# One TensorE order for a fused FFN, attention and RWKV-7 block: how ready steps are chosen, and which engine carries the small copies

## The chip, the cores and the metric

One core of a Trainium2 chip runs the whole program in one launch. The metric is device time in microseconds, the median of the runs shown; smaller is better.

## What is computed

Two models in a row on 256 tokens of width 1024, all in float32. The first block is an FFN (width 2816), a mixer, an FFN and a final norm. Its mixer projects the normed rows once and uses the columns for a dilated attention (12 heads), for an RWKV-7 time mix (16 heads of 64) and for two sets of gates. Then two layers of FFN, sparse and latent attention, FFN. The change lies in the first block's mixer. Of the reference, cut to it:

```python
def token_shift(z, mu):
    prev = jnp.pad(z, ((0, 0), (1, 0), (0, 0)))[:, :-1]
    return z + (prev - z) * mu

def hybrid_mixer(h, ...):
    proj = h @ w_in
    gates = jax.nn.sigmoid(proj[..., aw + rs:] + gate_bias)
    y_attn = dilated_attention(proj[..., :aw], positions) @ attn_w_up
    y_rwkv = rwkv7_time_mix(token_shift(proj[..., aw:aw + rs], rwkv_mu), ...)
    merged = gates[..., :D_MODEL] * y_attn + gates[..., D_MODEL:] * y_rwkv
    return merged @ w_o

# rwkv7_time_mix, per head: S_t = S_{t-1} diag(w_t) + (S_{t-1} a_t) b_t^T + v_t k_t^T ;  y_t = S_t r_t
```

## The kernel before, in words

**Stages.** The stages run one after the other: ffn f1, mix1, ffn f2, final, f3, mix2, f4, f5, mix2, f6, final. Products are made of three float32r matmuls each (high and low parts, `mm3`, L1799 to L1801; in the FFNs L1857 and L1859). Weights come in chunks of up to 1 MB through three `raw` buffers; ScalarE writes the high part (`split`, L2345), VectorE the low part (L2711), in four pieces a chunk.

**How the order is made.** The class `Order` writes one list of steps ahead of time; every engine then runs its share in order, and semaphores join them. In mix1 and mix2 the function `woven` interleaves chains: the first is `dense` (weight products), the others are the recurrence's. Each chain has a time at which its next step is ready, from the table `PACE` and from `HOP`; `woven` takes the first chain in the list that is ready, so `dense` comes first as soon as its rest of 1.0 us after its last step is over. `mode` says whether TensorE's last step was of 64-wide tiles (`QUARTERS`) or not. `BLANKS` names steps ahead of which TensorE runs so many matmuls on data that nobody reads (`fill`, L1808, 256 columns each).

**mix1.** First the qkv tile 0 with the norm, then two small shifted projections (`shift`, for the LoRA columns), then the rest of qkv; then attention, interleaved with gates 0 and 1 and the shifted k, v, r projections of group pair 0; then `rwkv`. There 8 head pairs g run as chains `group`, `decay`, `rows`, `gates`; two Front and three Whole buffers are shared among them. `dense` there is: `up` (attention output times its weights), `streams(1)` (shifted k, v, r of heads 2 and 3), gate 2, `streams(2)`, gate 3, `streams(3)`, and then `wout`. `streams(G)` waits until the rows of pairs 2G-4 and 2G-3 have been used. Each g has 20 steps of 64-wide tiles: `r_lora`, `r_pairs`, `r_dm0`, `r_g0`, five `r_x`, five `r_d`, `r_w`, `r_rp`, `r_yp`, three `r_s`; and full steps such as `r_norm`, `r_wide`, `r_vb`, `r_ka`, `r_bonus`, `r_mean`, `r_var`, `r_lg`, `r_turn2`.

**Around the changed operations.** A shift: `shift_mm` on TensorE into one PSUM bank; `shift_copy` on ScalarE copies the bank into the buffer `z` one column to the right (L2452) and frees the bank; `shift_mix` on VectorE subtracts (L2831, 128x512) and adds mu times the difference (L2836, twice). `r_key` ends with a VectorE copy that spreads a norm per head over 64 columns (L2959) for TensorE's `r_wide`; `r_wide2` does the same (L3093) ahead of `r_turn2`. `r_st` scales a 128x64 state out of PSUM (L3073, VectorE), three times a pair, and `r_s` on TensorE (L2157, L2159) waits for each.

```python
def shift_copy(s, sid, n, w):
    for t in due(("pe", ("shift", sid)), ("pool", ("z0",)), z_free(sid)):
        e.wait_ge(*t)
    e.activation(z[0:w, 0:n, 1:257], bank(sid)...[0:w, 0:n, :], copy)
```

Of the kernel before, what the change touches and what calls it, by code (L numbers as in the profile page):

```python
# [24 lines left out]
CW = 2048  # L25


def plan(stages):
# [11 lines left out]
    def body(s):  # L40
# [15 lines left out]
        elif s[0] == "mix1":  # L56
# [7 lines left out]
            out += gate[0] + gate[1] + kvr[0] + [("mix1", "up", 0, 2048)] + kvr[1] + gate[2] + kvr[2] + gate[3] + kvr[3]  # L64
# [30 lines left out]
def down_after(m):  # L95

    if 5 <= m <= 8:
# [11 lines left out]
    "r_key": (("dve", 0.59),), "r_wide": (("pe", 0.25),), "r_vb": (("pe", 0.45), ("act", 0.68)),  # L109
# [4 lines left out]
    "r_rp": (("pe", 0.35), ("dve", 0.69)), "r_yp": (("pe", 0.9), ("pool", 0.1, "aside")), "r_st": (("dve", 0.22),),  # L114
    "r_s": (("pe", 0.15),), "r_ys": (("act", 0.43),), "r_mean": (("pe", 0.43), ("dve", 0.36)), "r_sq": (("act", 0.36),),
    "r_var": (("pe", 0.3), ("dve", 0.1), ("pool", 1.0)), "r_wide2": (("dve", 0.32),), "r_lg": (("pe", 0.88),),
# [32 lines left out]
         "r_ka", "r_bonus", "r_pairs"}  # L149
HOP = {"pe": 0.3, "act": 0.1, "dve": 0.1, "pool": 0.15}  # L150
# [144 lines left out]
class Dry:  # L295
# [44 lines left out]
    def max(self, *a, **k):  # L340
        return self
# [3180 lines left out]
```

## Time and profile before

| | us |
|---|---|
| median of 3 runs | 1875.25 (1875.21 to 1876.46) |
| the profiled execution, its own time | 1876.75 |
| its span | 1875.0 |
| TensorE busy in the span | 1846.3 (98%) |
| VectorE, ScalarE, GpSimd busy | 1200.3, 1014.8, 91.2 |
| share of the last-ending chain on TensorE | 91% |
| blanks (L1808) over the whole span | 317 matmuls |

The profiled execution is 1.5 us over the median. Busy is the union of an engine's instructions; TensorE's matmuls are pipelined, so time lost between two kinds of matmul still counts as busy, and so do blanks. mix1's recurrence lies between 338 and 583 us of the span, its attention ahead of it, its output products behind it to about 640 us.

### The profile page before, as it was taken

The numbers are of one execution on the slowest core, as the hardware profiler recorded it, in microseconds if no ns is written. First come the engines' busy times: TensorE is split into PE (matmuls) and PEld (weight loads), VectorE is DVE, ScalarE is ACT, GpSimd is POOL, SyncE is SP. The second block draws the span as 40 slices with busy tenths as digits, with TensorE's granted clock in tenths as the row PEclk, the third lists the DMA queues.
The fourth block names the chain that finished last, engine by engine and source line by source line (L and its number), as shares of the span: only waits on it lengthen the run. The fifth ranks groups of instructions, "written<-read, shape, count | busy, mean of one in ns | idle before, by whom it ended". The sixth has DMA issues, their size and how long they took to land.

```text
span 1875.0 us, 31192 instructions
## 1 busy us (share of the span) xinstructions
PE 1846.3 (98%) x12765; PEld 1569.5 (84%) x12765; DVE 1200.3 (64%) x2485; ACT 1014.8 (54%) x2074; POOL 91.2 (5%) x187
## 2 busy tenths in 40 slices
PE   8999999999999999999999999999999999999998
PEld 7888888888887888888888887888888888878887
DVE  5666545767766557665666665667566767566565
ACT  5565455534523556555655765556555656655554
POOL 0000000211210000010001000000000000000000
PEclk9999999999999999999999999999999999999999
DMA  6556443222214356535652333556355634334552
GB/s 244 181 202 234 159 157 113 101 88 94 76 53 159 125 193 233 202 109 184 230 208 85 132 135 113 182 204 241 114 181 200 242 98 133 137 113 168 201 185 109
DMA packets 42719, 296.31 MB, mean 158 GB/s; under 512 B 4832, under 2 KB 4960, under 8 KB 10576
## 3 DMA queue, kind: packets, MB, share of 16 engines
q1 hardware_dynamic: 41184, 288.48, 43.5%
q0 software_dynamic: 1392, 5.83, 0.9%
q8 instruction: 101, 1.65, 0.4%
q14 instruction: 42, 0.34, 0.1%
HBM read 293.25 MB, written 1.05 MB: 157 GB/s over the span
## 4 chain that ended last, share of the span: by engine, by line
PE 91%; DVE 5%; ACT 2%; POOL 1%; issue 1%; DMA 1%; SPq 0%; POOLq 0%; DVEq 0%; ACTq 0%
PE PS L1857 22%; PE PS L1799 16%; PE PS L1801 15%; PE PS L1800 15%; PE PS L1859 11%; PE PS L1808 1%; PE PS L2100 1%; PE PS L2302 1%; PE PS L1834 1%; PE PS L2214 1%; DVE wlo L2711 1%; PE PS L1993 1%; PE PS L2266 1%; PE PS L2258 1%; PE PS L2081 1%
## 5 line engine op out<-in xcount | busy, mean ns | idle before, releaser
L2711 DVE TENSOR_TENSOR wlo<-raw,whi 128x512 fp32r<-128x512 f32 (+5 forms) x788 | 612.7, 823 | 191.7 <-ACT whi L2345 185.1
L1857 PE MATMUL PS<-xhl,whi 128*128 128x512 f32 x1728 | 612.9, 398 | 0.0
L2345 ACT ACTIVATE whi<-raw 128x512 fp32r<-128x512 f32 (+5 forms) x788 | 531.2, 731 | 144.1 <-PE PS L1801 144.0
L1859 PE MATMUL PS<-xhl,wlo 128*128 128x256 f32 x1728 | 484.8, 281 | 0.0
L1857 PEld LDWEIGHTS PS<-xhl,whi 128*128 128x128 f32 x1728 | 324.7, 188 | 79.1
L1859 PEld LDWEIGHTS PS<-xhl,wlo 128*128 128x128 f32 x1728 | 326.2, 189 | 2.1
L1799 PE MATMUL PS<-whi,yh 128*128 128x512 f32 (+2 forms) x572 | 224.9, 393 | 0.5 <-DVE yl L3115 0.3
L1801 PE MATMUL PS<-whi,yl 128*128 128x512 f32 (+2 forms) x572 | 221.8, 388 | 0.0
L1800 PE MATMUL PS<-wlo,yh 128*128 128x512 f32 (+2 forms) x572 | 221.7, 388 | 0.0
L1799 PE MATMUL PS<-whi,xhl 128*128 128x512 f32 (+4 forms) x480 | 191.5, 399 | 1.1 <-ACT arena L2546 0.7
L2796 DVE TENSOR_TENSOR arena<-arena,PS 128x256 f32<-128x256 f32 x216 | 90.3, 418 | 159.2 <-ACT arena L2415 159.2
L1801 PE MATMUL PS<-whi,xhl 128*128 128x512 f32 (+4 forms) x480 | 180.1, 375 | 0.0
L1800 PE MATMUL PS<-wlo,xhl 128*128 128x512 f32 (+4 forms) x480 | 179.9, 375 | 0.0
L1799 PEld LDWEIGHTS PS<-whi,yh 128*128 128x128 f32 x572 | 107.4, 188 | 26.0 <-issue 3.1
L1801 PEld LDWEIGHTS PS<-whi,yl 128*128 128x128 f32 x572 | 107.4, 188 | 23.1
L1800 PEld LDWEIGHTS PS<-wlo,yh 128*128 128x128 f32 x572 | 107.5, 188 | 19.5
L2412 ACT ACTIVATE arena<-arena 128x256 f32<-128x256 f32 x108 | 45.1, 418 | 124.7 <-DVE arena L2796 124.7
L1799 PEld LDWEIGHTS PS<-whi,xhl 128*128 128x128 f32 x480 | 90.6, 189 | 17.7 <-issue 2.4
L1801 PEld LDWEIGHTS PS<-whi,xhl 128*128 128x128 f32 x480 | 90.5, 188 | 14.0
L2418 ACT ACTIVATE yh<-arena 128x256 fp32r<-128x256 f32 x108 | 45.1, 418 | 102.3 <-DVE arena L2800 102.3
L1800 PEld LDWEIGHTS PS<-wlo,xhl 128*128 128x128 f32 x480 | 90.8, 189 | 11.3
L2804 DVE TENSOR_TENSOR yl<-arena,yh 128x256 fp32r<-128x256 f32 x108 | 46.0, 425 | 52.3 <-ACT yh L2418 52.3
(269 smaller groups left out, 2400.6 us busy)
## 6 DMA issues: line engine op xcount, KB each, us to landing
raw<-wall SPq DMA_DIRECT2D x249, 1024.0 KB, 4.9
raw<-wall SPq DMA_DIRECT2D x12, 768.0 KB, 4.3
raw<-wall SPq DMA_DIRECT2D x8, 968.0 KB, 4.9
raw<-wall SPq DMA_DIRECT2D x4, 896.0 KB, 4.7
arena<-ebias POOLq DMA_DIRECT2D x2, 768.0 KB, 4.7
raw<-wall SPq DMA_DIRECT2D x2, 720.0 KB, 4.1
raw<-wall SPq DMA_DIRECT2D x2, 640.0 KB, 4.5
X<-x SPq DMA_DIRECT2D x2, 512.0 KB, 5.9
```

Source lines behind the costliest of these rows:

```text
L1799: e.matmul(o, wa, xa, start=first, stop=False)
L1800: e.matmul(o, wa, xb, start=False, stop=False)
L1801: return e.matmul(o, wb, xa, start=False, stop=last)
L1808: e.matmul(PS[:, i, 0:256], still[:, 0:128], still[:, :], start=True, stop=True)
L1857: e.matmul(b, hi[:, c0:c0 + 128], xhl[:, k, :, :].rearrange("p a t -> p (a t)"), start=(k == 0), stop=False, skip_group_check=True)
L1859: p = e.matmul(b[:, 0:256], lo[:, c0:c0 + 128], xh[:, k, :], start=False, stop=(k == 7), skip_group_check=True)
L2345: e.activation(whi[slot_of(i)][:, c].bitcast(F32R), raw[i % 3][:, c], copy).then_inc(*M.sig("whi", ("split", i, q)))
L2412: e.activation(g, g, ACT.Silu).then_inc(*M.sig("act", ("silu", s, m)))
L2418: e.activation(hbuf(m)[0], g, copy).then_inc(*M.sig("act", ("hh", s, m)))
L2711: e.tensor_tensor(wlo[slot_of(i)][:, c], raw[i % 3][:, c], whi[slot_of(i)][:, c].bitcast(F32), ALU.subtract).then_inc(*M.sig("wlo", *[("ha ...
L2796: e.tensor_tensor(o, o, bank(("gu", s, m, n))[:, 0:256], ALU.add).then_inc(*M.sig("dve", (key, s, m), ("free", ("gu", s, m, n))))
L2804: e.tensor_tensor(hl, g, hh.bitcast(F32), ALU.subtract).then_inc(*M.sig("dve", ("hl", s, m)))
```

## The change

It has seven parts.

1. `woven` keeps the name of each chain's last step; among the chains that are ready it prefers one whose next TensorE step is of the tile that TensorE is in (`NEXTQ` names the last steps after which a 64-wide one comes).
2. `dense` of `rwkv` follows the table `DENSE`: k, v, r of pair group 1, `up`, groups 2 and 3, gates 2 and 3. The chunks of weights are loaded in that order.
3. The shift has no buffer `z`: ScalarE writes (1 - mu) times the bank straight into its place, in two instructions; VectorE adds mu times the bank one column to the right, out of PSUM, and frees the bank. The wait for the place (`kzv_free`) moves from VectorE to ScalarE. 1 - mu is made once (`m1_begin`); the memset of `z` goes.
4. `r_st` moves from VectorE to ScalarE.
5. The two spreads (in `r_key`, and `r_wide2`) move from VectorE to ScalarE.
6. `PACE` has new estimates for these steps.
7. `BLANKS` has other entries: 146 matmuls in mix1 for 195, none for 4 in the first FFN, 50 for 49 in each mix2.

```diff
+DENSE = (('kvr', 1, 1.0), ('up', 0, 1.0), ('kvr', 2, 1.0), ('kvr', 3, 1.0), ('gate', 2, 1.0), ('gate', 3, 1.0))
...
-            out += gate[0] + gate[1] + kvr[0] + [("mix1", "up", 0, 2048)] + kvr[1] + gate[2] + kvr[2] + gate[3] + kvr[3]
+            out += gate[0] + gate[1] + kvr[0]
+            for what, n, _ in DENSE:
+                out += {"up": [("mix1", "up", 0, 2048)], "gate": gate[n], "kvr": kvr[n]}[what]
...
-    "shift_mm": (("pe", 1.54),), "shift_copy": (("act", 0.54),), "shift_mix": (("dve", 1.47),),
+    "shift_mm": (("pe", 1.54),), "shift_copy": (("act", 0.7),), "shift_mix": (("dve", 0.86),),
...
+NEXTQ = {"r_dt", "r_dm0", "r_xc", "r_dd", "r_w", "r_rp", "r_yp", "r_st", "r_s", "r_scaled", "r_bonus"}
...
-    ('proj', 0, 'gh', 0, 4): 4, ('turn_x', 1, 0, 0): 4, ('proj', 1, 'qkv', 1, 0): 4, ('proj', 1, 'gate', 0, 0): 13,
-    ('att_qk', 1, 0): 15, ('att_turn', 1, 1, 1, 0): 3, ('att_out', 1, 3, 0): 8, ('up', 1, 0, 0, 0): 20,
-    ('r_vb', 1, 0): 8, ('r_vb', 1, 1): 9, ('r_g0', 1, 1): 5, ('r_g0', 1, 2): 5, ('r_d', 1, 5, 1): 6,
-    ('r_g0', 1, 6): 6, ('r_dm0', 1, 6): 13, ('r_turn2', 1, 5): 5, ('r_d', 1, 7, 3): 11, ('r_x', 1, 7, 5): 3,
-    ('r_s', 1, 7, 1): 4, ('r_s', 1, 7, 2): 4, ('r_s', 1, 7, 3): 4, ('r_mean', 1, 7): 4, ('r_var', 1, 7): 8,
-    ('r_turn2', 1, 7): 5, ('wout', 1, 3, 1, 0): 19, ('wo', 1, 1, 0, 1): 6, ('wo', 1, 3, 0, 0): 3,
+    ('turn_x', 1, 0, 0): 4, ('proj', 1, 'gate', 0, 0): 13, ('att_qk', 1, 0): 15, ('att_out', 1, 3, 0): 8,
+    ('r_vb', 1, 0): 14, ('r_d', 1, 4, 1): 7, ('r_dm0', 1, 5): 6, ('r_s', 1, 4, 3): 4, ('r_g0', 1, 7): 9,
+    ('r_d', 1, 7, 4): 5, ('r_d', 1, 7, 5): 4, ('r_s', 1, 7, 1): 4, ('r_s', 1, 7, 2): 3, ('r_s', 1, 7, 3): 3,
+    ('r_mean', 1, 7): 4, ('r_var', 1, 7): 7, ('r_turn2', 1, 7): 6, ('wout', 1, 3, 1, 0): 19,
+    ('turn_merged', 1, 4, 0): 4, ('wo', 1, 1, 0, 1): 7, ('proj', 4, 'gh', 0, 0): 20, ('turn_x', 5, 0, 0): 4,
...
-            c = next((c for c in able if max(c[1], c[3]) <= self.now), None) or min(able, key=lambda c: max(c[1], c[3]))
+            now = [c for c in able if max(c[1], c[3]) <= self.now]
+            c = next((c for c in now if (c[4] in NEXTQ) == self.mode), None) or (now and now[0]) or min(able, key=lambda c: max(c[1], c[3]))
...
+            c[4] = self.steps[-1][0] if len(self.steps) > n else c[4]
...
         self.do("shift_copy", s, sid, n, w)
-        self.bank.give(sid)
         yield 1
         self.do("shift_mix", s, sid, n, w)
+        self.bank.give(sid)
...
             def shift_copy(s, sid, n, w):
-                for t in due(("pe", ("shift", sid)), ("pool", ("z0",)), z_free(sid)):
+                o, b = dest(sid), bank(sid)
+                for t in due(("pe", ("shift", sid)), ("dve", ("less",)), *kzv_free(sid)):
                     e.wait_ge(*t)
...
+                for j in range(n):
+                    e.activation(o[0:w, j, :], b[0:w, j * 256:(j + 1) * 256], copy, scale=less(mus(sid)[j])[0:w]).then_inc(
+                        *M.sig("act", ("shift", sid)))
...
+            def r_st(s, g, c):
+                W_, q, tt = WH[slot("whole", g)], c % 2, c // 2
+                for t in due(("pe", ("s", g, c) if c else ("yp", g)), ("act", ("pc", g))):
+                    e.wait_ge(*t)
+                e.activation(W_.ST[:, c, :], bank(("YP", g, q))[:, 128 + tt * 64:192 + tt * 64], copy,
+                             scale=W_.st[:, 24 + c:25 + c]).then_inc(*M.sig("act", ("ST", g, c)))
+
+            def r_wide2(s, g):
+                W_ = WH[slot("whole", g)]
+                for t in due(("pool", ("rsd", g))):
+                    e.wait_ge(*t)
+                e.activation(u4(W_.B), W_.st[:, 4:8].unsqueeze(2).to_broadcast([128, 4, 64]), copy).then_inc(
+                    *M.sig("act", ("wide2", g)))
...
             def shift_mix(s, sid, n, w):
-                o = dest(sid)
-                for t in due(("act", ("shift", sid)), *kzv_free(sid), COLS):
-                    e.wait_ge(*t)
-                e.tensor_tensor(o[0:w, 0:n, :], z[0:w, 0:n, 0:256], z[0:w, 0:n, 1:257], ALU.subtract).then_inc(
-                    *M.sig("dve", ("shifted", sid)))
+                o, b = dest(sid), bank(sid)
+                for t in due(("act", ("shift", sid)), COLS):
+                    e.wait_ge(*t)
                 for j in range(n):
...
+                    e.scalar_tensor_tensor(o[0:w, j, 1:256], b[0:w, j * 256:j * 256 + 255], col("mu", mus(sid)[j])[0:w],
+                                           o[0:w, j, 1:256], ALU.mult, ALU.add).then_inc(
+                        *M.sig("dve", ("mix", sid), *[("free", sid)] * (j == n - 1)))
```

## Rows read from the trace of the kernel before

**Rows 1.** the page's part 1: busy time, share, instructions
```profile
PE 1846.3 (98%) x12765; PEld 1569.5 (84%) x12765; DVE 1200.3 (64%) x2485; ACT 1014.8 (54%) x2074; POOL 91.2 (5%) x187
```

**Rows 2.** stretches of mix1: length, busy us (x instructions) by engine, PEclk, DMA
```profile
338.00:510.00 172.00, 168.80 (x2906) 144.40 (x2906) 129.69 (x340) 76.71 (x188) 40.64 (x59) 1.00 0.26 90
510.00:548.00 38.00, 35.69 (x1008) 30.98 (x1005) 29.09 (x97) 11.39 (x33) 6.67 (x14) 1.00 0.04 11
```

**Rows 3.** TensorE in order of time, 13 to 18 us
```profile
16.98 0.74 PE L1808 MATMUL PS<-still 128*128 128x256 f32 x4 [1.53 <-ACT still L2336]
17.56 0.39 PE L1799 MATMUL PS<-early,xhl 128*128 128x512 f32 x1
```

**Rows 4.** VectorE in the same stretch
```profile
14.78 1.28 DVE L2711 TENSOR_TENSOR early<-raw,early 128x512 fp32r<-128x512 f32 x2
```

**Rows 5.** TensorE around the first qkv tile after the lora shifts
```profile
223.37 0.63 PE L1808 MATMUL PS<-still 128*128 128x256 f32 x4
224.19 0.50 PE L1799 MATMUL PS<-whi,xhl 128*128 128x512 f32 x1 [0.19 <-DVE wlo L2711]
```

**Rows 6.** TensorE before the up product
```profile
330.38 2.63 PE L1808 MATMUL PS<-still 128*128 128x256 f32 x20
333.28 0.47 PE L1799 MATMUL PS<-whi,yh 128*128 128x512 f32 x1 [0.27 <-DVE small L2936]
```

**Rows 7.** TensorE around 64-wide steps, 391 to 397 and 567 to 569 us
```profile
395.81 0.67 PE L2109 MATMUL PS<-arena 64*64 64x128 f32 x16
396.30 0.38 PE L2081 MATMUL PS<-arena 64*64 64x32 f32 x16
...
566.92 0.39 PE L1800 MATMUL PS<-wlo,yh 128*128 128x512 f32 x1
567.14 0.39 PE L1801 MATMUL PS<-whi,yl 128*128 128x512 f32 x1
567.46 0.67 PE L2109 MATMUL PS<-arena 64*64 64x128 f32 x16
568.06 0.50 PE L1799 MATMUL PS<-whi,yh 128*128 128x512 f32 x1
568.39 0.40 PE L1800 MATMUL PS<-wlo,yh 128*128 128x512 f32 x1
```

**Rows 8.** TensorE in order of time: first and last 64-wide stretch of the recurrence
```profile
339.28 0.70 PE L1981 MATMUL PS<-arena 64*128 64x256 f32 x4
...
575.62 0.33 PE L2159 MATMUL PS<-arena 64*64 64x64 f32 x4
```

**Rows 9.** blanks (L1808) of two stretches: TensorE busy us (x instructions)
```profile
338.00:600.00 262.00, 19.55 (x125) 16.14 (x125) 1.00 0.24 84
```

**Rows 10.** TensorE's waits, 330 to 600 us: in total, times, longest
```profile
PE PS L1993 <- DVE arena L2959: 1.2, 1, 1.2
```

**Rows 11.** VectorE by line, 330 to 600 us: busy, mean ns, idle before
```profile
L2831 DVE TENSOR_TENSOR arena<-arena 128x512 f32<-128x512 f32 x10 | 6.9, 691 | 5.9 <-ACT arena L2452 5.9
L3073 DVE TENSOR_SCALAR arena<-PS,arena 128x64 f32<-128x64 f32 x24 | 6.7, 281 | 10.7 <-PE PS L2159 5.5 <-PE PS L2146 5.0
...
L2959 DVE COPY arena<-arena 128x256 f32<-128x256 f32 x8 | 2.5, 314 | 0.0
```

**Rows 12.** ScalarE by line, 330 to 600 us
```profile
L2452 ACT ACTIVATE arena<-PS 128x512 f32<-128x512 f32 x10 | 6.0, 599 | 27.7 <-PE PS L1801 27.7
...
L2573 ACT ACTIVATE arena<-PS 128x128 f32<-128x128 f32 x16 | 3.6, 275 | 11.8 <-PE PS L2159 11.7
...
L2585 ACT ACTIVATE yh<-arena 128x256 fp32r<-128x256 f32 x8 | 3.3, 414 | 16.1 <-DVE arena L3108 16.1
...
L2542 ACT ACTIVATE arena<-PS 128x256 f32<-128x256 f32 x8 | 3.1, 384 | 4.0 <-PE PS L1993 3.7
...
L2532 ACT ACTIVATE arena<-arena 128x4 f32<-128x4 f32 x8 | 1.6, 195 | 0.0
```

**Rows 13.** one stretch at a lower granted clock (PEclk)
```profile
1134.00:1138.00 4.00, 4.00 (x19) 3.48 (x17) 1.21 (x2) 0.90 (x2) 0.00 (x0) 0.57 0.72 305
```

More of the change, by code:

```diff
@@ L610, in woven @@
         self.epochs.append(len(self.steps))
-        live, idle = [[g, self.now, False, 0.0] for g in (steady,) + chains], 0
+        live, idle = [[g, self.now, False, 0.0, ""] for g in (steady,) + chains], 0
         dense = live[0]
@@ L1010, in dense @@
         def dense():
-            self.acc(s, "up")
-            yield from self.down("up", s, lambda j: ("mix1", "up", 0), [0], True)
-            self.do("gate_attn", s)
-            self.acc_free(s, "up")
-            yield from streams(1)
-            yield from self.gate(s, 2)
-            yield from streams(2)
-            yield from self.gate(s, 3)
-            yield from streams(3)
+            for what, n, self.rest in DENSE:
+                if what == "up":
+                    self.acc(s, "up")
+                    yield from self.down("up", s, lambda j: ("mix1", "up", 0), [0], True)
+                    self.do("gate_attn", s)
+                    self.acc_free(s, "up")
+                elif what == "gate":
+                    yield from self.gate(s, n)
+                else:
+                    yield from streams(n)
             while not set(range(6)) <= out:
@@ L1574, in build @@
         KZV[0] = {q: sp.take(2, 256) for q in "kvr"}
-        LW, z = sp.take(1024), sp.take(2, 257)
+        LW = sp.take(1024)
         sp = Space()
@@ L1718, in dest, with kzv_free, less @@
             return KZV[sid[1] % 2][sid[0]]
-        def z_free(sid):
-            q, G = sid
-            if q == "l":
-                return G and ("dve", ("mix", ("l", 0)))
-            if q == "k":
-                return "dve", ("mix", ("r", G - 1) if G else ("l", 1))
-            return "dve", ("mix", ({"v": "k", "r": "v"}[q], G))
+        def kzv_free(sid):
+            if sid[0] == "l":
+                return []
+            return marked("kzv", sid[1] - 2) if sid[1] >= 2 else marked("attn", 1) if sid[1] else marked("norm", 1)
+        def less(j):
+            return small[:, 16 + j:17 + j]
         def mus(sid):
@@ L2001, in r_wide @@
             def r_wide(s, g):
-                for t in due(bank_free(("r_wide", g)), ("dve", ("wide", g))):
+                for t in due(bank_free(("r_wide", g)), ("act", ("wide", g))):
                     e.wait_ge(*t)
@@ L2151, in r_s @@
                 b = bank(("YP", g, q))
-                for t in due(("dve", ("Ph", g)), ("dve", ("ST", g, c - 1))):
+                for t in due(("dve", ("Ph", g)), ("act", ("ST", g, c - 1))):
                     e.wait_ge(*t)
@@ L2182, in r_turn2 @@
             def r_turn2(s, g):
[L2183 removed]
+                for t in due(bank_free(("r_turn2", g)), ("act", ("wide2", g))):
                     e.wait_ge(*t)
@@ L2566, in r_w, with r_key @@
                     *M.sig("act", ("w", g), *freed("r_w", g)))
+            def r_key(s, g):
+                F_ = FR[slot("front", g)]
+                for t in due(("pool", ("nrm", g))):
+                    e.wait_ge(*t)
+                e.activation(u4(F_.wide), F_.st.unsqueeze(2).to_broadcast([128, 4, 64]), copy).then_inc(
+                    *M.sig("act", ("wide", g)))
+            def r_st(s, g, c):
[10 more added lines that the diff above has]
+                    *M.sig("act", ("wide2", g)))
             def r_ys(s, g):
@@ L2956, in r_key @@
                 e.scalar_tensor_tensor(F_.kp, F_.kp, 1.0, k3, ALU.add, ALU.mult).then_inc(*M.sig("dve", ("kp", g)))
-                for t in due(("pool", ("nrm", g))):
-                    e.wait_ge(*t)
-                e.tensor_copy(u4(F_.wide), F_.st.unsqueeze(2).to_broadcast([128, 4, 64])).then_inc(
-                    *M.sig("dve", ("wide", g)))
             def r_scaled(s, g, part):
@@ L3067, in r_rp @@
                     *M.sig("dve", ("Ph", g), ("free", ("RP", g, 0))))
-            def r_st(s, g, c):
-                W_, q, tt = WH[slot("whole", g)], c % 2, c // 2
-                for t in due(("pe", ("s", g, c) if c else ("yp", g)), ("act", ("pc", g))):
-                    e.wait_ge(*t)
-                e.tensor_scalar(W_.ST[:, c, :], bank(("YP", g, q))[:, 128 + tt * 64:192 + tt * 64],
-                                W_.st[:, 24 + c:25 + c], None, ALU.mult).then_inc(*M.sig("dve", ("ST", g, c)))
             def r_mean(s, g):
```

45 lines of the change are left out of this document (17 added, 28 removed).

## The prediction

> **What bounds the kernel now.** I read the engines' busy time first: TensorE is busy 98% of the span [rows 1], so only what shortens TensorE's own line counts, or what lets it wait less. Next the stretches of mix1: while the recurrence runs beside products (338 to 510 us) TensorE is busy 168.80 of 172 us, and in the part where no products are left (510 to 548 us) 35.69 of 38; VectorE is busy three quarters of both, ScalarE 45% and 30% [rows 2]. VectorE is thus the second engine and ScalarE has room. Busy TensorE hides three kinds of loss, and the change aims at all: open waits, blanks, and changes between 64-wide and full steps. Open waits are small: the longest of the recurrence is 1.2 us, on the spread L2959 [rows 10]. Between 338 and 600 us blanks take 19.55 us in 125 matmuls, 0.156 us each with the entry to their batch [rows 9]; a blank more in a batch costs 0.12 to 0.15 us (20 in 2.63) [rows 6]. Changes of tile are read from start times.
>
> **The price of a 64-wide stretch.** Full fp32r matmuls of 512 columns stand 0.23 us apart (566.92 to 567.14 and its like). From the one at 567.14 to the 64-wide step behind it 0.32 pass, so entering costs 0.09; the first full matmul after it (568.06) takes 0.33 to the next, so leaving costs 0.10 [rows 7]. The step itself, L2109, takes 0.60 when it stands alone (567.46 to 568.06) and 0.49 when another 64-wide step follows (395.81 to 396.30) [rows 7]: 0.11 of waiting for the last ones to drain. A stretch less saves 0.09 + 0.10 + 0.11 = **0.30 us**. In the order of starts I count 88 stretches with the 160 64-wide steps of the recurrence, from 339.28 to 575.62 us [rows 8]: 1.8 steps each.
> The Trainium skill ("TensorEngine Tiling (Array Packing)", Key Properties) says that a change of tiling mode drains the TensorE; it gives no figure, and the trace agrees. By that rule every merged pair would save the whole 0.30, whatever stands beside it, and the sum would be the one below.
>
> **The change part by part.**
> *Start.* In the first FFN the four blanks wait for a constant from ScalarE until 16.98, and the product behind them starts at 17.56 [rows 3]; the half chunk it needs was cut by 14.78 + 1.28 = 16.06 on VectorE [rows 4]. Without blanks it starts about 16.1: **-1.4 us**. The chunks behind it are fed ahead of TensorE, which shows no wait after that point before the tile's end; if one of them is late, the gain is 0.
> *First qkv tile.* Four blanks end at 224.00 and the product still waits 0.19 for the low part [rows 5]. VectorE's queue had the subtraction of the shift ahead of it, 0.69 us [rows 11], which goes; ScalarE's two copies add at most 2 x 0.384 - 0.599 = 0.17 ahead of the high part [rows 12]. **-0.5**, ends 0 and -0.8.
> *up.* After the turn of the attention's output, TensorE runs 20 blanks and waits until 333.28, 2.90 us from 330.38, for that output's low part [rows 6]. In the new order shifted k of group 1 stands there, which needs only normed rows and weights; its chunk takes the place of up's in the loading. The attention's end is then covered by 18 us of products. **-2.9**, other end 0 if k's chunk is late.
> *Order of ready steps.* Stretches of 1.8 steps can at best become about 3 (three Whole buffers, so three pairs under way, one ready step each): 160/3 = 53 stretches, 35 less, -10.5. At worst no second step is ready at a choice: 88 and 0. A 1.4 us product step lets all three chains become ready, which speaks for the far half, the dependence of every step on VectorE or ScalarE for the near one. I take the middle, 18 less: 18 x 0.30 = **-5.4**.
> *Gates last.* 22 us of gate products move from between the shifts to the end, where the stretch without products stands with its blanks and waits; they cover it, while the shifts, closer together, start the later pairs sooner. What of the blanks goes: 106 for 125 between 338 and 600 us (up's 20 lie ahead of it), 19 x 0.12 = **-2.3**; ends 0 (the stall is still there, uncovered) and 19 x 0.156 = -3.0. Three more go in the attention and three in wo: **-0.5**. The chain of the last pair (its `r_s`, mean, variance, turn, then wout with 19 blanks) stays bare in either order.
> *Shift without z.* Per shift VectorE loses 0.69 [rows 11], over ten shifts of the stretch 6.9; its two other operations stay. ScalarE gains 0.17. The bank is freed by VectorE and not by ScalarE, about 1 us later, in 8 banks; cover is that products rest 1.0 us between steps. The wait for the place goes ahead of ScalarE's copy; behind it stand the high parts of weights and the recurrence's copies. Nothing before shows VectorE waiting at L2831 for anything but ScalarE's copy (5.9 us in all) [rows 11], so I cost it at 0.
> *Spreads and states.* VectorE loses 24 x 0.281 and 16 spreads of about 0.31 [rows 11], 11.8 us; with the shifts 18.6 us of the 194 that it is busy there. For a 128x64 copy out of PSUM ScalarE has no row: between 0.195 (128x4) and 0.275 (128x128) [rows 12], against 0.281; I take 0.25, equal on the chain. A spread on ScalarE is nearest to its 128x256 copy inside SBUF, 0.414 [rows 12]: 0.1 longer than now, 16 times, bare only for the last pair. What VectorE no longer has in its queue ends most of the wait for L2959 (1.2) [rows 10]: **-1.0**, ends 0 and -1.2. Added on the other side: `r_st` or a spread behind a piece of the weights' high part on ScalarE, which takes 0.6 as the bank copy does; counted in the range.
> The Trainium skill ("VectorE: DVE Perf Modes", the TRN2 errata) speaks against the spreads' move: its fixed cost for a source in SBUF is 224 cycles at 1.2 GHz on ScalarE and 58 at 0.96 GHz on VectorE. By it a spread would be 0.40 us there and 0.33 here, an estimate from that page; the trace has 0.414 and 0.314 and agrees in direction, and 16 x 0.1 us on the path would turn the sum by 1.6 us at most.
> *Two mix2 stages.* One blank more each: **+0.2**.
>
> **Sum.** 1.4 + 0.5 + 2.9 + 5.4 + 2.3 + 0.5 + 1.0 - 0.2 = 13.8 us off. The profiled execution took 1876.75 (span 1875.0), 1.5 over the median; the savings are inside the span and I take them from the median: 1875.25 - 13.8 = **1861.5**.
>
> **Rivals.**
> *A: the chains set the time.* Each pair's 20 steps depend on one another; if TensorE has less to do per step, it waits more, and the merged stretches and dropped blanks come back as waits. For it: already now no products are left at 510 to 548 us and 2.3 us are open there [rows 2]. Against: with products TensorE is open only 3.2 of 172 us [rows 2]. Only start, qkv and up stay: 4.8 off, **1870.5**.
> *B: the order rule merges nothing* (the change does not do what it says), because seldom two steps are ready; all else holds: 13.8 - 5.4 = 8.4 off, **1866.9**.
> *C: slower, products run out in the middle.* `streams(2)` and `streams(3)` wait for rows of earlier pairs, and no gate stands between them now. TensorE then runs recurrence steps alone. Such a stretch wastes 2.3 us open and about 5.3 in 44 blanks (0.12 each) in 38, a fifth. Before it is 38 us long; the gates at the end win these 7.6 back. If the bare stretches ahead of both shift groups last L us, the loss is 0.2 L; with no merging and no dropped blank (1870.5 as in A) the point of decision is 0.2 L - 7.6 = 4.8, L = 62 us. With 80 us the time is 1870.5 - 7.6 + 16 = **1879**. For it: the group of heads 4 and 5 can only be shifted once pair 1's rows are used; against: the shifts themselves are 17 us each.
> Also, one stretch of 4 us runs at a mean granted clock of 0.57 [rows 13], in a mix2 stage that the change leaves as it is; the lower level (1.2 GHz) there followed TensorE's small attention steps and a wait. It costs six matmuls 0.2 us more each; it may go or come again: 1.2 us either way, for the range.
>
> **How the numbers follow.** About 0.2% (3.75 us) is what a measurement of this kernel can tell from no change. Forecast 0.65, A 0.16, B 0.10, C 0.09. The forecast's own range: merging at its far end and blanks and start at theirs 5.1 + 0.9 more, the clock 1.2: 1854; down to near B, 1868. Eight in ten takes in A with its bounds: 1853 to 1872. Faster (below 1871.5): all of the forecast, 0.09 of A's 0.16, 0.06 of B's 0.10 (its blanks can fail with it): 0.80. Same: 0.07 + 0.04 = 0.11. Slower: C, 0.09.
>
> **What the changed profile would show.** Right: no blank ahead of the first FFN's fifth k; a shift product at 330 us where blanks stood; clearly under 88 stretches of 64-wide steps, about 70; 0.30 for each that went; gate products beside the recurrence's last pairs; VectorE 18 us less busy and ScalarE some 14 more; spreads at 0.41 on ScalarE. Wrong: open waits of TensorE in the recurrence over 10 us in sum (A); a count near 88 (B); tens of microseconds with no fp32r matmul before the third shift group (C); ScalarE's shift copy waiting for GpSimd, VectorE or a chain's rows; a product waiting for a chunk that is not cut.

## The result, and the profile after

The changed kernel takes **1862.39 us** (median of 5 runs, 1861.97 to 1873.29) against 1876.05 us (1875.21 to 1877.22) for the kernel before in the same comparison: a ratio of 0.9939 [0.9924, 0.9953], 13.7 us less. The forecast was 13.8 us less, 1861.5.

The execution that was profiled with it is the longest of the five, 1873.29 us (span 1871.5), 11 us over its median, so its trace alone would tell another story than the time. The same kernel went to the chip once more (`e1_again`: 1861.78 us in the profiled execution, span 1860.0), and that trace is the one to lay beside the kernel before. Every line number of TensorE's program is 8 higher than before: products L1807 to L1809, blanks L1816. First the page's busy times of `e1_again`, columns as in [rows 1].

```profile
PE 1833.8 (99%) x12714; PEld 1562.2 (84%) x12714; DVE 1182.0 (64%) x2432; ACT 1029.0 (55%) x2127; POOL 89.2 (5%) x186
```

TensorE is 12.5 us less busy, VectorE 18.3 less, ScalarE 14.2 more. Next the recurrence, which from here on is the stretch from the turn of the attention's output (L1826 before, L1834 now) to the last group of `wout`. The view is the stretches, columns as in [rows 2]: the kernel before, then `e1_again`, then the first trace of the changed kernel with the stretch in it that ran at half clock.

```profile
330.03:584.23 254.20, 247.98 (x4240) 211.35 (x4239) 179.67 (x485) 102.91 (x251) 50.69 (x78) 1.00 0.24 85
```
```profile
327.80:570.60 242.80, 237.35 (x4197) 205.17 (x4197) 163.51 (x435) 116.96 (x301) 48.81 (x78) 1.00 0.25 88
```
```profile
329.20:580.80 251.60, 246.29 (x4197) 212.34 (x4196) 163.49 (x435) 117.03 (x301) 48.87 (x78) 0.96 0.24 86
526.20:546.60 20.40, 20.33 (x268) 16.84 (x265) 8.37 (x24) 5.62 (x14) 2.41 (x4) 0.50 0.17 60
```

So 11.4 of the 15.0 us between the spans are saved here: 254.2 us became 242.8 (the window's edges are rounded; from start to start it is 242.7, as in the table below). In the first trace of the changed kernel the same 4197 matmuls took 251.6, because for 20.4 us of them the granted clock was 0.50 (1.2 GHz). Half of 20.4 is 10.2, and 251.6 - 242.8 is 8.8.

The start, and the place where `up`'s 20 blanks stood [rows 3, 6], TensorE in order of time in `e1_again`:

```profile
14.72 0.40 PE L1809 MATMUL PS<-early,xhl 128*128 128x512 f32 x1
15.80 0.50 PE L1807 MATMUL PS<-early,xhl 128*128 128x512 f32 x1 [0.68 <-DVE early L2742]
...
222.03 0.50 PE L1807 MATMUL PS<-whi,xhl 128*128 128x512 f32 x1 [0.16 <-DVE wlo L2742]
...
327.85 0.60 PE L1834 MATMUL PS<-C,arena 128*128 128x128 f32 x4
328.20 0.36 PE L1807 MATMUL PS<-xhl,whi 128*128 128x256 f32 x1
```

The fifth k starts at 15.80 (17.56 before), with nothing ahead of it but the wait for the cut chunk; the first qkv tile at 222.03 (224.19). Behind the attention's turn a shift product starts after 0.35 us, at 328.20, where the next product stood 3.25 us behind (330.03 to 333.28).

Merged steps, TensorE in order of time in `e1_again`:

```profile
399.26 0.59 PE L2174 MATMUL PS<-arena,C 128*128 128x256 f32 x2
399.78 1.08 PE L2154 MATMUL PS<-arena 64*64 64x64 f32 x53
400.65 0.25 PE L2101 MATMUL PS<-arena 64*64 64x32 f32 x2
...
400.96 0.63 PE L2108 MATMUL PS<-arena 64*64 64x32 f32 x15
401.53 0.61 PE L1995 MATMUL PS<-C,arena 128*128 128x2 f32 x4
```

Two 64-wide steps of different pairs stand side by side here: `r_yp` (L2154) and an `r_d`, which has two groups of matmuls (L2101, L2108). Counted in the order of starts, the 160 64-wide steps stand in **70 stretches** where there were 88, and 21 of these are a single step where 45 were.

The end of the products, TensorE in order of time: the last product of the shifts and the first of `wout` before, then the last of the gates and the first of `wout` in `e1_again`.

```profile
508.37 0.28 PE L1801 MATMUL PS<-xhl,wlo 128*128 128x256 f32 x1
...
548.48 0.58 PE L1799 MATMUL PS<-whi,yh 128*128 128x512 f32 x1
```
```profile
510.97 0.40 PE L1809 MATMUL PS<-whi,xhl 128*128 128x512 f32 x1
...
534.34 0.59 PE L1807 MATMUL PS<-whi,yh 128*128 128x512 f32 x1
```

For 40.1 us no product stood beside the last pairs' steps; now it is 23.4.

What the moved operations cost, ScalarE by line from 325 to 590 us, then VectorE (columns as in [rows 11]):

```profile
L2462 ACT ACTIVATE arena<-PS,small 128x256 f32<-128x256 f32 x20 | 8.4, 469 | 18.9 <-PE PS L1809 18.9
L2589 ACT ACTIVATE arena<-PS,arena 128x64 f32<-128x64 f32 x24 | 7.5, 312 | 24.6 <-PE PS L2167 13.2 <-PE PS L2154 11.4
...
L2596 ACT ACTIVATE arena<-arena 128x256 f32<-128x256 f32 x8 | 3.3, 413 | 5.7 <-POOL arena L3357 5.6
...
L2582 ACT ACTIVATE arena<-arena 128x256 f32<-128x256 f32 x8 | 3.3, 411 | 0.7 <-POOL arena L3339 0.7
```
```profile
L2865 DVE SCALAR_TENSOR_TENSOR arena<-PS,C,arena 128x255 f32<-128x255 f32 x20 | 8.7, 474 | 5.6 <-ACT arena L2462 5.5
```

The shift's copies (L2462) wait for TensorE alone, 18.9 us in all, and never for a place or for VectorE; the mix (L2865) waits 5.6 us, all but 0.1 of it for them, as L2831 did before (5.9) [rows 11].

### The profile page after: what moved, and what is told of

Same layout as the page of the kernel before. It is cut to its first block, busy times and chain, and to the rows that moved or that the text cites. A ratio compares the mean times of both kernels' runs of the same rounds, so it can differ in the third digit from the quotient of the medians.

```text
span 1871.5 us, 31118 instructions
## 1 busy us (share of the span) xinstructions
PE 1844.7 (99%) x12714; PEld 1570.5 (84%) x12714; DVE 1181.7 (63%) x2432; ACT 1029.5 (55%) x2127; POOL 89.4 (5%) x186
## 4 chain that ended last, share of the span: by engine, by line
PE 91%; DVE 4%; ACT 3%; DMA 1%; issue 1%; POOL 1%; SPq 0%; POOLq 0%; DVEq 0%; ACTq 0%
PE PS L1865 22%; PE PS L1807 16%; PE PS L1809 15%; PE PS L1808 15%; PE PS L1867 11%; PE PS L1816 1%; PE PS L2108 1%; DVE wlo L2742 1%; PE PS L2310 1%; PE PS L1842 1%; PE PS L2222 1%; PE PS L2089 1%; PE PS L2274 1%; PE PS L2266 1%; PE PS L2101 1%
## 5 line engine op out<-in xcount | busy, mean ns | idle before, releaser
L1807 PE MATMUL PS<-whi,yh 128*128 128x512 f32 (+2 forms) x572 | 225.8, 395 | 0.4 <-DVE yl L3127 0.3
L1808 PE MATMUL PS<-wlo,yh 128*128 128x512 f32 (+2 forms) x572 | 222.4, 389 | 0.0
L1809 PE MATMUL PS<-whi,yl 128*128 128x512 f32 (+2 forms) x572 | 222.4, 389 | 0.0
L1807 PE MATMUL PS<-whi,xhl 128*128 128x512 f32 (+4 forms) x480 | 191.4, 399 | 0.3 <-DVE wlo L2742 0.3
L1809 PE MATMUL PS<-whi,xhl 128*128 128x512 f32 (+4 forms) x480 | 179.9, 375 | 0.0
L1808 PE MATMUL PS<-wlo,xhl 128*128 128x512 f32 (+4 forms) x480 | 179.6, 374 | 0.0
L1807 PEld LDWEIGHTS PS<-whi,yh 128*128 128x128 f32 x572 | 107.8, 189 | 26.2 <-issue 2.6
L1809 PEld LDWEIGHTS PS<-whi,yl 128*128 128x128 f32 x572 | 107.8, 188 | 23.2
L1808 PEld LDWEIGHTS PS<-wlo,yh 128*128 128x128 f32 x572 | 107.9, 189 | 19.7
L1807 PEld LDWEIGHTS PS<-whi,xhl 128*128 128x128 f32 x480 | 90.6, 189 | 16.4 <-DVE wlo L2742 1.4
L1809 PEld LDWEIGHTS PS<-whi,xhl 128*128 128x128 f32 x480 | 90.3, 188 | 14.1
L1808 PEld LDWEIGHTS PS<-wlo,xhl 128*128 128x128 f32 x480 | 90.8, 189 | 11.3
L2423 ACT ACTIVATE arena<-PS 128x256 f32<-128x256 f32 x108 | 40.7, 377 | 70.7 <-PE PS L1867 70.7
```

What stands on the lines that cost most here:

```text
L1807: e.matmul(o, wa, xa, start=first, stop=False)
L1808: e.matmul(o, wa, xb, start=False, stop=False)
L1809: return e.matmul(o, wb, xa, start=False, stop=last)
L2423: e.activation(up, bank(("gu", s, m, 1))[:, 256:512], copy).then_inc(*M.sig("act", ("up2", s, m)))
```

## The experiments

Times are medians, ratios are against the kernel before, run beside it on the same chip (medians 1875.5 to 1876.0 us; `e1` to `e4`, `e5` to `e8` and `e9` to `e12` each had a chip of their own). A trace shows one execution out of four or more: those of `e3` and `e10` took 2.3 and 4.2 us less than their median, that of `e8` 3.2 us more. For every run I read the recurrence in the same six numbers. **Length** and the time at **half clock** are read from the trace (PEclk 0.50 by stretches); **open** is all of TensorE's waiting in the recurrence in gaps over 0.15 us, in front of steps and of blanks and inside steps (the sum of the view of its waits); **blanks** are matmuls of the filler; **stretches** are runs of 64-wide steps, both counted in the order of starts; **bare** is the sum of the stretches of 11 us and more in which no product step starts.

```
kernel                        time    length  half clock  open  blanks  stretches  bare
before                        1876.05  254.2     0         5.3    139      88      54.8
after, first trace            1862.39  251.6    20.5       5.0     95      70      44.2
e1  after again               1862.37  242.7     0         5.1     95      70      37.3
e2  no rule                   1876.75  256.7    10.2       9.3     95      85      49.6
e3  old product order         1893.23  270.9    27.3      18.8     95      72      66.8
e4  r_st, spreads back        1880.75  261.4    20.4      15.3     88      70      60.2
e5  no rule, blanks fitted    1868.11  248.6     0         3.8    106      89      49.1
e6  old order, blanks fitted  1886.88  267.3    23.9       7.2    154      82      62.5
e7  back, blanks fitted       1875.79  256.3     0         6.4    161      74      56.7
e8  no blanks before r_       1865.60  248.7    20.4      12.9     19      61      37.7
e9  before + rule             1887.81  266.3    17.1      15.2    133      74      67.0
e10 before + copies           1888.82  265.5    17.1      11.4    128      85      66.5
e11 before + product order    1886.14  264.4    13.7      12.3    123      86      63.5
e12 warmer start              1862.82  242.9     0         4.9     95      70      37.1
```

One sum fits nearly all rows: length = 205 + open + 0.12 per blank + 0.30 per stretch + half of the time at half clock. The two prices are those of the prediction, and 205 is what is left of a row on average: 254.2 - 5.3 - 16.7 - 26.4 = 205.8 in `before`, 242.7 - 5.1 - 11.4 - 21.0 = 205.2 in `e1`. Over all rows it misses by 1.0 us at most, but for `e7`, which is 3.4 longer. Fitted freely to the other thirteen rows (least squares, open taken as it is), the prices come out at 0.12 for a blank, 0.32 for a stretch and 0.47 of the time at half clock, so the rows bear the prediction's two prices out.

**Bare** is no term of that sum, since it holds waits, blanks and stretches itself, but it sorts the kernels nearly as their times do: 37 us in the changed kernel and without the pairs' blanks, 49 to 50 without the rule, 55 before, 57 and 60 with the copies back, 62.5 to 67 in all others; the first trace, with its half-clock stretch, has 44. It follows the times and doesn't show what makes them.

### The changed kernel again

The kernel is unchanged, five runs.

> The changed kernel once more, nothing edited. Its median was 1862.39 us while its one profiled execution took 1873.29 with 20.4 us at half clock in the recurrence. If that half-clock stretch is chance, this run gives 1862 +- 1 and a profile without it, span near 1860.5. If it belongs to being profiled or to this order, the profile shows it again at the same place (526 to 547 us).

Measured: 1862.37 us (1861.41 to 1866.57), 0.9933 [0.9919, 0.9947]. The gain is the same on a second comparison. The long stretch at half clock and the one at the start are both absent from this trace, and one run of the five is again 4 us above the others. The stretch of the first trace therefore belongs to an execution and not to the kernel.

### Without the rule

```diff
-            c = next((c for c in now if (c[4] in NEXTQ) == self.mode), None) or (now and now[0]) or min(...)
+            c = (now and now[0]) or min(...)
```

> The changed kernel with the old choice among ready chains (first in the list). Its order has 85 stretches of 64-wide steps where the changed kernel has 70. Theory (each stretch costs 0.30 us): 15 x 0.30 = 4.5 us more, 1866.9. Rival A (chains set the time, merged stretches come back as waits): no change, 1862 to 1863, with TensorE's open waits in the recurrence smaller by what the stretches cost more.

Measured: 1876.75 us (1873.5 to 1879.24), 1.0004 [0.9995, 1.0013]; the whole gain is gone. Stretches go from 70 to 85, worth 4.5 us, yet the time goes up by 14.4. The trace has the rest: 4.2 us more open, and two stretches at half clock that `e1` doesn't have, worth 5.1. The three make 13.8 of the 14.0 us that the recurrence is longer.

```profile
431.00:434.40 3.40, 3.40 (x32) 3.06 (x25) 2.04 (x4) 1.42 (x3) 1.56 (x3) 0.50 0.00 0
540.30:547.10 6.80, 6.63 (x71) 5.14 (x64) 3.99 (x9) 3.24 (x8) 0.31 (x1) 0.50 0.00 0
```

The blanks in this kernel are still those written for the order that the rule gives; in another order they stand ahead of steps that are ready, and the waits are elsewhere. So the run doesn't price the rule alone, which is why `e5` follows.

### With the products' old order

```diff
-DENSE = (('kvr', 1, 1.0), ('up', 0, 1.0), ('kvr', 2, 1.0), ('kvr', 3, 1.0), ('gate', 2, 1.0), ('gate', 3, 1.0))
+DENSE = (('up', 0, 1.0), ('kvr', 1, 1.0), ('gate', 2, 1.0), ('kvr', 2, 1.0), ('gate', 3, 1.0), ('kvr', 3, 1.0))
```

> The changed kernel with the products in the old order (up, kvr 1, gate 2, kvr 2, gate 3, kvr 3); 72 stretches. Theory: the wait ahead of up is back, 2.9 us (now open, no blanks), the stretch without products is bare again, 2.3, and two stretches more, 0.6: 5.8 more, 1868.2. Rival (only up mattered, the gates' place not): 2.9, 1865.3. Rival C turned round (gates between helped): under 1865.

Measured: 1893.23 us (1890.92 to 1896.56), 1.0094 [1.008, 1.0108]: 31 us more than the changed kernel, and 17 more than the kernel before, which has this same order. Waits of TensorE from 327.7 to 598.7 us (in total, times, longest), and the product of `up` behind the attention's turn:

```profile
PE PS L2001 <- ACT arena L2596: 2.3, 2, 1.3
PE PS L2001 <- DVE arena L3004: 2.2, 3, 1.7
PE PS L1807 <- DVE small L2966: 2.2, 1, 2.2
PE PS L2067 <- DVE arena L3051: 1.9, 1, 1.9
PE PS L2130 <- ACT arena L2575: 1.6, 3, 0.7
```
```profile
330.50 0.47 PE L1807 MATMUL PS<-whi,yh 128*128 128x512 f32 x1 [2.15 <-DVE small L2966]
```

The wait that `up`'s 20 blanks filled [rows 6] is back as 2.15 us of open time: the third line of the waits. Another 12 us are waits of up to 1.9 us on the pairs' steps (18.8 us open for 5.1 in all), and 27.3 us run at half clock. Behind the last shift no product starts for 34.0 us, and then again for 20.5 and 12.3: the gates no longer cover the last pairs.

### r_st and the spreads back on VectorE

```diff
-            def r_st(s, g, c):
...
-                e.activation(W_.ST[:, c, :], bank(...), copy, scale=W_.st[:, 24 + c:25 + c])
+            def r_st(s, g, c):
...
+                e.tensor_scalar(W_.ST[:, c, :], bank(...), W_.st[:, 24 + c:25 + c], None, ALU.mult)
...
-                e.activation(u4(F_.wide), F_.st.unsqueeze(2).to_broadcast([128, 4, 64]), copy)
+                e.tensor_copy(u4(F_.wide), F_.st.unsqueeze(2).to_broadcast([128, 4, 64]))
```

The lines taken out are ScalarE's and those put in VectorE's. `r_wide2` likewise; `PACE` gets its old estimates for the three steps.

> The changed kernel with r_st and both spreads back on VectorE; 70 stretches as before. Theory: 1.0 us more, 1863.4, and VectorE 11.8 us busier. Rival (VectorE is the true second bound, so its relief made the merging possible): 3 us or more, 1865.5 or over. Rival (a copy on ScalarE is slower on the chain): the time falls below 1862.

Measured: 1880.75 us (1880.18 to 1882.2), 1.0028 [1.0017, 1.0039], 18 us more than the changed kernel. VectorE is 10.6 us busier in the recurrence (174.12 for 163.51), and TensorE waits for it:

```profile
PE PS L2089 <- DVE arena L3057: 2.4, 1, 2.4
PE PS L2001 <- DVE arena L3102: 2.1, 1, 2.1
PE PS L2001 <- DVE arena L2987: 1.9, 2, 1.0
PE PS L2101 <- DVE arena L3117: 1.6, 1, 1.6
PE PS L2117 <- DVE arena L3062: 1.5, 3, 0.9
```

That is a term 18 times the size that I gave it. But the stretches (70) are the same as in `e1`, so what grew is waiting (10.2 us) and half clock (20.4, worth 10.2).

### The three again, each with blanks fitted to it

The entries of `BLANKS` that lie in the recurrence are replaced in each: where that kernel's own trace shows a wait of 0.33 us or more (blanks taken away), one blank for every 0.125 us of it. From `e5`, the lines joined:

```diff
-    ('r_vb', 1, 0): 14, ('r_d', 1, 4, 1): 7, ('r_dm0', 1, 5): 6, ('r_s', 1, 4, 3): 4, ('r_g0', 1, 7): 9,
...
+    ('r_vb', 1, 0): 16, ('r_g0', 1, 3): 8, ('r_d', 1, 5, 1): 5, ('r_d', 1, 5, 5): 5, ('r_rp', 1, 5): 4,
...
```

> e2 (old choice among ready chains) with the blanks of the recurrence put where e2's own profile has TensorE waiting 0.33 us or more, one per 0.125 us. Theory after e2: its 14.4 us over the changed kernel are half-clock stretches (10.2 us long, 5.1 lost), open waits that the table didn't cover, and only 4.5 for 15 more stretches of 64-wide steps. Then blanks that fit bring the clock back: 1867.5 to 1869. Rival: the clock doesn't fall for lack of blanks, and the order alone costs 14: 1875 to 1877 again.

> e3 (products in the old order) with blanks fitted to its own profile in the same way. TensorE's waits in e3, with blanks taken away, add up to 22.5 us in the recurrence against 13.7 in e1: 8.8 more. Theory: 8.8 plus up to 3.6 for stretches, clock back: 1871 to 1875. Rival (the blanks have no part in it): 1891 to 1895 again.

> e4 (state scaling and spreads back on VectorE) with blanks fitted to its own profile. Waits with blanks taken away: 21.3 us in e4, 13.7 in e1, 7.6 more, nearly all on VectorE. Theory (VectorE is the second bound): 1862.4 + 7.6 + about 1 for stretches: 1870 to 1872. Rival 1 (as in the prediction, the copies cost 1.0 and all else in e4 was the clock): 1863.5 to 1865. Rival 2 (blanks have no part): 1880 to 1882 again.

Measured: `e5` 1868.11 us (1867.74 to 1869.78), 0.9961 [0.9948, 0.9975]; `e6` 1886.88 (1884.31 to 1887.43), 1.0056 [1.0044, 1.0069]; `e7` 1875.79 (1874.53 to 1878.58), 1.0 [0.9991, 1.0009]. `e5` came out as expected, `e6` and `e7` above their theories' ranges (1871 to 1875 and 1870 to 1872) and below the rivals in which blanks have no part. The recurrence of `e5`, `e6` and `e7`, columns as above:

```profile
328.10:576.70 248.60, 243.98 (x4208) 207.65 (x4207) 164.35 (x435) 117.79 (x301) 50.65 (x78) 1.00 0.24 87
```
```profile
328.40:595.70 267.30, 259.60 (x4256) 221.88 (x4255) 165.56 (x437) 117.49 (x302) 50.57 (x78) 0.96 0.24 84
```
```profile
329.00:585.30 256.30, 249.09 (x4263) 214.41 (x4262) 173.79 (x477) 105.92 (x262) 50.06 (x78) 1.00 0.25 88
```

Fitting alone gives back 8.6, 6.3 and 5.0 us, and in `e5` and `e7` every stretch at half clock in the recurrence is gone (PEclk 1.00). What is left over the changed kernel is the price of each part in this setting, and an upper bound: each table was fitted once, from one trace, and no run fits the changed kernel's own table anew in the same way, so part of a price can be a worse fit.

- **The rule: 5.7 us.** 19 stretches more (89 for 70) at 0.30 are 5.7; 11 blanks more (1.3) and 1.3 us less open cancel. No half clock is in the way here, and it is the prediction's price.
- **The product order: 24.5 us**, of which 59 blanks are 7.1, 12 stretches 3.6, 2.1 is open and 12.0 is half of 23.9 us at half clock. Blanks didn't cure this order: 62.5 us stay bare, and with 154 blanks it still has waits and the low clock. `e6` has the rule and the copies of the changed kernel on the product order of the kernel before, and is 11 us slower than that kernel: in the old order the two gain nothing even with blanks fitted to them once.
- **r_st and the spreads: 13.4 us**, of which 66 blanks are 7.9, 4 stretches 1.2 and 1.3 is open. The other 3 are not accounted for. `r_st` and the spreads were only moved together, so what each is worth stays open.

### Without the blanks ahead of the pairs' steps

```diff
-    ('r_vb', 1, 0): 14, ('r_d', 1, 4, 1): 7, ('r_dm0', 1, 5): 6, ('r_s', 1, 4, 3): 4, ('r_g0', 1, 7): 9,
-    ('r_d', 1, 7, 4): 5, ('r_d', 1, 7, 5): 4, ('r_s', 1, 7, 1): 4, ('r_s', 1, 7, 2): 3, ('r_s', 1, 7, 3): 3,
-    ('r_mean', 1, 7): 4, ('r_var', 1, 7): 7, ('r_turn2', 1, 7): 6,
```

> The changed kernel without the 76 blanks ahead of the recurrence's steps (those ahead of wout, wo, gates and attention stay); order and everything else the same. Theory (blanks only keep the clock up): TensorE's waits are as long as before, now open, half-clock stretches of several us come in the recurrence, 1868 to 1878. Rival (blanks cost what they hide): no half-clock stretch, and 0 to 1 us faster than 1862.4.

Measured: 1865.60 us (1862.51 to 1868.77), 0.9948 [0.9935, 0.996]: 3.2 us more than with them by the medians, though the intervals of the two ratios overlap (`e1` has 0.9919 to 0.9947); the expectation had 1868 to 1878, or no more than 1862.4. The 76 blanks cost 9.1 us of TensorE; without them 7.8 us more is open and, blanks no longer cutting them, only 61 stretches are left. At full clock this kernel would be the faster one, by an estimate that no run shows: 248.7 - 10.2 is 238.5, against 242.7. But in this trace, of the longest of its five executions, it runs 20.4 us at half clock, in four places:

```profile
341.00:344.40 3.40, 3.40 (x18) 3.40 (x17) 3.33 (x10) 2.02 (x5) 0.00 (x0) 0.50 0.54 227
392.20:399.00 6.80, 6.80 (x92) 6.07 (x91) 3.23 (x9) 1.35 (x4) 2.23 (x2) 0.50 0.02 7
453.60:457.00 3.40, 3.40 (x25) 3.27 (x21) 1.43 (x4) 2.55 (x7) 0.96 (x3) 0.50 0.02 5
569.70:576.50 6.80, 6.76 (x27) 5.95 (x28) 1.97 (x5) 0.83 (x2) 1.04 (x1) 0.50 0.00 0
```

Read this way, a blank fills a wait and shortens none, and what it is worth is the clock behind the wait: a few us in all.

### Each part alone on the kernel before

`e9` adds the rule (the line of `e2`, and `NEXTQ`), `e10` the shift without `z`, `r_st` and the spreads on ScalarE, with the old choice and the old product order, `e11` the new product order:

```diff
+            now = [c for c in able if max(c[1], c[3]) <= self.now]
+            c = next((c for c in now if (c[4] in NEXTQ) == self.mode), None) or (now and now[0]) or min(...)
```
```diff
-            yield from streams(1)
-            yield from self.gate(s, 2)
-            yield from streams(2)
-            yield from self.gate(s, 3)
-            yield from streams(3)
+            for what, n, self.rest in DENSE:
```

All three keep the old table of blanks. A blank is written only where a PSUM bank is free at that place of the order, so not all of the 139 come: 133, 128 and 123.

> The kernel before with the new choice among ready chains alone; 74 stretches of 64-wide steps for 88, its blanks as before. Theory (the parts add up, 0.30 us a stretch): 14 x 0.30 = 4.2 off, 1871.5. Rival (the parts only pay together: blanks and estimates of before don't suit the new order): 1875 to 1882, with more open waits and half-clock stretches than before.

> The kernel before with the shift without z, the state scaling and the spreads on ScalarE, and their estimates; old choice, old order of products, blanks of before. Theory of the prediction: 0.5 + 1.0 off, 1874.3. After e7 (13.4 us lost when scaling and spreads go back to VectorE) the rival is that VectorE's relief is worth the same here: 1862 to 1866. Rival 2: only in the new order, where VectorE is pressed harder, is it worth anything: 1874 to 1880.

> The kernel before with the new order of products and chunks alone (k, v, r of group 1 ahead of up; gates last), blanks of before without the 20 ahead of up, which find no free bank or no step there. Theory of the prediction: 2.9 + 2.3 off, 1870.5 or a little over, since its blanks aren't fitted. Rival (shifts closer together press VectorE, which carries 18 us more here): waits in the recurrence grow, 1876 to 1885.

Measured: `e9` 1887.81 us (1886.16 to 1891.06), 1.0068 [1.0056, 1.0081]; `e10` 1888.82 (1884.14 to 1891.67), 1.0069 [1.0055, 1.0083]; `e11` 1886.14 (1883.89 to 1886.43), 1.0054 [1.0041, 1.0066]. All three lie above the ranges of their rivals too. **Each of the three parts of a change that gains 13.7 us loses 11 to 13 when it is made alone, with the old blanks.** Waits of TensorE in the recurrence of `e9`, then of `e11`:

```profile
PE PS L1996 <- DVE arena L3096: 2.1, 1, 2.1
PE PS L1996 <- DVE arena L2981: 1.7, 3, 0.9
PE PS L2084 <- DVE arena L3111: 1.5, 1, 1.5
```
```profile
PE PS L2106 <- DVE arena L3044: 2.1, 2, 1.4
PE PS L2115 <- DVE arena L3054: 1.0, 1, 1.0
```

`e9` merges as it should (88 to 74 stretches, 4.2 us), and loses it to 10 us more open and 17.1 at half clock. `e10` has VectorE's relief and the kernel before's product order, and no gain either. `e11` alone has the short stretch behind the gates (22.9 us without a product, as 23.8 in `e1`), but two more of 15.3 and 11.6 elsewhere: the cover has moved and the chains have not come under it. And the 20 blanks of `up`, which the expectation took to be gone, run at the new place of `up`, behind a wait for the bank that they write:

```profile
370.59 2.66 PE L1814 MATMUL PS<-still 128*128 128x256 f32 x20 [0.69 <-ACT arena L2542]
```

In each kernel the order of the steps has moved, and its 123 to 133 blanks stand in places fitted to another. Whether one of them would gain with blanks of its own wasn't tried: only the three kernels of the section before had them fitted.

### A longer warm-up

```diff
-        self.do("warm", 10)
+        self.do("warm", 15)
...
-                if n < 12:
+                if n != 12:
```

The second pair keeps VectorE's part of this warm-up empty, as it was.

> The changed kernel with 5 more warm-up matmuls ahead of the first product, into the wait of 1.2 to 2.3 us there. In e4, e7, e8 and the first profile a half-clock stretch of 3.4 us begins at 13 to 14 us and the first qkv tile starts 1.0 us later than in the profiles without. Theory: the stretch doesn't come, 0.5 to 1 us off in the mean and less spread: 1861.5. Rival: the first product is held up by the warm-up itself: 1862.5 to 1863.

Measured: 1862.82 us (1860.55 to 1863.55), 0.993 [0.9917, 0.9942], the same as the changed kernel. The first trace of the changed kernel has 3.4 us at half clock from 14.2 us, and so have `e4`, `e7` and `e8` near there; in this trace the stretch is absent, and so it is in `e1`, `e2`, `e3`, `e5` and `e6`, without the longer warm-up; so this doesn't show that the warm-up keeps it away. Where it comes, the attention's turn starts at 328.9 to 329.2 us; in `e1`, `e2`, `e3`, `e5`, `e6` and `e12` at 327.7 to 328.4, so it costs some 1 us. No version came out ahead of the changed kernel.

## Why the prediction was right, and where its reasons were not

The time and most of its terms held. That the sum meets the median to 0.1 us is partly luck: between the two traces 15.0 us are saved and not 13.8, of which 1.5 is a half-clock stretch of a mix2 stage that one of them has, and the 18 stretches of the largest term are the middle of bounds 35 apart. What failed is the idea that they could be had one by one. Against the trace of the kernel before, by `e1_again`'s starts:

- **Start**, -1.4: the fifth k starts 1.76 us earlier, and 1.66 is left from the next product on. It waits 0.68 for its cut chunk, which is the bound that the step named.
- **First qkv tile**, -0.5: 2.16 us ahead at that point, so 0.5 of it here. At the attention's turn it is 2.18: the three attention blanks gave nothing. wo's neither: 13.6 us ahead before it, 13.5 behind.
- **up**, -2.9: the turn to the next product took 3.25 us and takes 0.35, so 2.9. `e3` put `up` back and got the wait of 2.15 without its blanks. Blanks and wait together are the term.
- **Order of ready steps**, -5.4: 70 stretches, as taken from the middle of the bounds, and 5.7 us for 19 of them in `e5`. The Trainium skill's rule that a change of tiling mode drains TensorE ("TensorEngine Tiling (Array Packing)", Key Properties) agrees with `e5`, where 19 changes into 64-wide steps and back cost their full 0.30 us each.
- **Blanks**, -2.3: 106 stand between 325 and 590 us for the 125 of [rows 9], 19 less.
- **Shift without z**, 0: L2865 waits as L2831 did, and no copy waits for a place. One copy took 0.469 and not 0.384, the copies that scale by a column being the longer ones (`r_st`, 128x64, took 0.312 where a plain 128x128 took 0.275 [rows 12]), so ScalarE got 0.34 more per shift, not 0.17; the mix waited no longer for it (5.6 us in all for 5.9).
- **mix2**, +0.2: not to be seen; the spans show 1.5 us the other way, the stretch of [rows 13] being at full clock in `e1`. In the first trace it is there again, 3.4 us at PEclk 0.50.

The recurrence lost 11.5 us where up, order, blanks and spreads made 11.6. By the table that is 0.2 open, 5.3 for 44 blanks (the 20 of `up` among them) and 5.4 for 18 stretches, 10.9.

**Where the reasoning failed.** *Spreads and states*, "-1.0, ends 0 and -1.2": 13.4 us when they are taken back with blanks fitted, 18 without. I read their worth from the one wait that they end now, L2959, and took VectorE's 75% [rows 2] for slack. In the order of the changed kernel 10.6 us more on VectorE leaves 56.7 us bare for 37.3: I read this as chains that come late, when the products that should cover them are used up; the waits of `e4` on VectorE fit it, and 3 us of the 13.4 are unexplained. The same relief on the old order was worth nothing with the old blanks (`e10`) and, with the rule, nothing with fitted ones (`e6`), so it is no price of the copies but of copies, order and blanks together. *Gates last*, "-2.3": the term held as the number of blanks dropped. But taking the order back costs 24.5 us with blanks fitted, 2.9 of it up: 21.6 us at most, 12.0 of them half clock, that the step had in its words ("they cover it") and not in its number. It counted the blanks that go and not the time without products that goes, 54.8 to 37.3 us. And the prediction treated the table of blanks as so many times 0.12 us. It is a table for one order of steps: under any other, its matmuls stand before ready steps and the real waits are bare, and half clock came in all eight runs with over 7 us open.

**Prices of single steps.** `r_st` took 0.312 on ScalarE for my 0.25, and 0.281 before, so it is slower there; a spread 0.411 and 0.413 for my 0.414. The Trainium skill's warning on such copies out of SBUF ("VectorE: DVE Perf Modes", the TRN2 errata) is borne out as far as the single instruction goes (0.314 on VectorE) and not in the time: `e7`, which heeds it, is 13.4 us longer, though it takes back `r_st`, which reads PSUM, as well.

**The rivals.** A: open time stayed where it was, 5.1 us for 5.3; over 10 was its mark. Rival A is out for this change, but the chains are close behind the products: `e3`, `e4` and `e9`, each with a part missing, have 15 to 19 us open. B: 70 stretches, not 88. C: in `e1` the longest time without a product step ahead of the third shift group's end is 6.0 us; it wanted over 62. *The clock*, "1.2 us either way": too small. The changed kernel's ten runs hold one 11 us above the median, whose trace has 20.4 us at half clock, and one 4 us above.

## What to carry to other kernels

In a kernel with an order written out and fillers fitted to it, a part tried alone also measures how badly the fillers now fit (5.0 to 8.6 us here): refit them for each variant before a verdict, and the unchanged kernel's in the same way. Fitted or not, parts need not add up. An engine that is busy three quarters of the time beside dependent chains was no slack in this kernel; what it was worth to relieve it couldn't be read from the one wait that the profile showed, and the time that the chains run without a product beside them followed it better. And a profiled execution 11 us above its median calls for a second trace before any stretch of it is explained.

## What the runs showed of the hardware

**Long stretches at half clock can follow short waits among small matmuls, in one execution and not in the next.** Just ahead of the stretch at 526.2 us in the first trace of the changed kernel, TensorE had run 32- and 64-column steps and waited twice for 0.8 us:

```profile
521.75 0.36 PE L2101 MATMUL PS<-arena 64*64 64x32 f32 x10 [0.81 <-issue]
...
526.03 0.59 PE L2101 MATMUL PS<-arena 64*64 64x32 f32 x16 [0.83 <-DVE arena L3079]
```

The granted clock then was 0.50 until 546.6, though TensorE was busy 20.33 of these 20.4 us, and the loss was about half of it. `e1`, the same program with as much waiting (5.1 us open for 5.0), ran there at 1.00; the second of the two waits was 0.56 us in it:

```profile
526.20:546.60 20.40, 19.85 (x266) 16.92 (x266) 10.70 (x27) 7.67 (x19) 3.15 (x4) 1.00 0.26 92
```

In the fourteen traces of this study such stretches, the one at the very end of a kernel apart, last from 3.4 to 20.5 us. The traces with little open time in the recurrence (`before`, `e1`, `e5`, `e7`, `e12`: at most 6.4 us) had none there; those over 7 us all had. The first trace (5.0) had one too, so that is no sharp line, and why one execution is granted the full clock and the next is not stays open.
